# Half-wide moving operands in the levels of a triangular inverse (chunked delta rule, one core)

## The reference

```python
L = jnp.where(strict, jnp.einsum('bhnid,bhnjd->bhnij', k_beta, kc) * decay, 0.0)
T = lax.linalg.triangular_solve(eye + L, jnp.broadcast_to(eye, L.shape),
                                left_side=True, lower=True, unit_diagonal=True)
v_corr = jnp.einsum('bhnij,bhnjd->bhnid', T, v_beta)
k_cumdecay = jnp.einsum('bhnij,bhnjd->bhnid', T, k_beta * jnp.exp(gc)[..., None])
```

## Time and profile before

| | us |
|---|---|
| median of 3 runs | 3319.24 |
| lowest, highest | 3318.76, 3329.38 |
| profiled execution, time | 3317.98 |
| profiled execution, span | 3315.7 |
| PE busy | 3227.7 (97%) |
| PE weight loads busy | 2680.6 (81%) |
| DVE busy | 2195.3 (66%) |
| ACT busy | 773.8 (23%) |

### The profile page before, as it was taken

How to read it: one execution, slowest core, us unless ns; L and a number is a source line. 1 busy time by engine, 2 the same in 40 slices (tenths; PEclk the granted TensorE clock), 3 DMA queues, 4 the chain that set the end, 5 groups by cost and what they waited for, 6 DMA issues and landing times.

```text
span 3315.7 us, 40252 instructions
## 1 busy us (share of the span) xinstructions
PE 3227.7 (97%) x15737; PEld 2680.6 (81%) x15737; DVE 2195.3 (66%) x3316; ACT 773.8 (23%) x1248; POOL 1834.9 (55%) x994
## 2 busy tenths in 40 slices
PE   6999999999999999999999999999999999999999
PEld 5787778887877887888888888888878887888887
DVE  6975389963336257564755888788854337888884
ACT  2152322211224122333121111255531011111110
POOL 4547367766541653012666666633356666777775
PEclk9999999999999999999999999999999999999999
DMA  3223122322320221000333444455553336556662
GB/s 132 84 64 102 53 92 97 96 96 89 111 73 26 94 78 58 14 20 31 119 106 117 140 140 138 134 200 207 204 185 105 123 121 208 186 190 200 199 194 99
DMA packets 164525, 391.67 MB, mean 118 GB/s; under 512 B 10865, under 2 KB 69489, under 8 KB 162289
## 3 DMA queue, kind: packets, MB, share of 16 engines
q1 hardware_dynamic: 73408, 262.70, 24.0%
q10 hardware_dynamic: 90928, 126.39, 11.3%
HBM read 326.14 MB, written 62.91 MB: 117 GB/s over the span
## 4 chain that ended last, share of the span: by engine, by line
PE 84%; DVE 11%; issue 2%; ACT 1%; DMA 1%; POOL 0%; DVEq 0%; ACTq 0%; POOLq 0%
PE banks L1519 22%; PE banks L1521 22%; PE banks L1520 22%; PE banks L909 3%; DVE sb_sq L2226 3%; PE banks L802 1%; PE banks L794 1%; PE banks L378 1%; DVE sb_tmp L2236 1%; DVE sb_sq L2224 1%; PE banks L1581 1%; PE banks L1555 1%; PE banks L1557 1%; PE banks L1556 1%; DVE sb_zL L546 1%
## 5 line engine op out<-in xcount | busy, mean ns | idle before, releaser
L1507 POOL TENSOR_TENSOR sb_wL<-sb_raw,sb_wH 128x1024 fp32r<-128x1024 f32 x495 | 1207.5, 2439 | 1454.1 <-PE banks L1521 1401.8
L1519 PE MATMUL banks<-sb_hH,sb_wH 128*128 128x512 f32 x2040 | 820.0, 402 | 12.9 <-ACT sb_sq L1124 3.1
L1520 PE MATMUL banks<-sb_hL,sb_wH 128*128 128x512 f32 x2040 | 796.7, 391 | 0.0
L1521 PE MATMUL banks<-sb_hH,sb_wL 128*128 128x512 f32 x2040 | 796.6, 390 | 0.0
L1502 POOL TENSOR_SCALAR sb_wH<-sb_raw 128x1024 fp32r<-128x1024 f32 x495 | 643.0, 1299 | 14.9 <-DMA sb_raw<-in_weights 14.9
L1519 PEld LDWEIGHTS banks<-sb_hH,sb_wH 128*128 128x128 f32 x2040 | 384.9, 189 | 97.6 <-issue 12.6
L1521 PEld LDWEIGHTS banks<-sb_hH,sb_wL 128*128 128x128 f32 x2040 | 383.8, 188 | 81.3
L1520 PEld LDWEIGHTS banks<-sb_hL,sb_wH 128*128 128x128 f32 x2040 | 385.0, 189 | 73.2 <-issue 1.7
L1519 PE MATMUL banks<-sb_pzH,sb_wH 128*128 128x512 f32 x1024 | 399.8, 390 | 5.9 <-DVE sb_xT L1471 3.8
L1521 PE MATMUL banks<-sb_pzH,sb_wL 128*128 128x512 f32 x1024 | 398.9, 390 | 0.0
L1520 PE MATMUL banks<-sb_pzL,sb_wH 128*128 128x512 f32 x1024 | 398.9, 390 | 0.0
(11 more groups left out here) (432 smaller groups left out, 4623.6 us busy)
## 6 DMA issues: line engine op xcount, KB each, us to landing
sb_raw<-in_weights SPq DMA_DIRECT2D x495, 512.0 KB, 3.7
gates<-sb_stage ACTq DMA_DIRECT2D x16, 2048.0 KB, 7.8
acts<-sb_sq ACTq DMA_DIRECT2D x96, 256.0 KB, 2.0
sb_Gt<-gates ACTq DMA_DIRECT2D x24, 1024.0 KB, 7.5
sb_Ga<-acts ACTq DMA_DIRECT2D x24, 1024.0 KB, 11.1
sb_Gt<-gates ACTq DMA_DIRECT2D x4, 2048.0 KB, 9.8
sb_xT<-in_xT SPq DMA_DIRECT2D x4, 512.0 KB, 9.9
acts<-sb_xT ACTq DMA_DIRECT2D x1, 2048.0 KB, 7.8
```

The source lines that it names most:

```text
L1507: nc.gpsimd.tensor_tensor(wL[:, t % LOS, :], raw[:, t % RAWS, :], wH[:, t % HIS, :].bitcast(F32), ALU.subtract).then_inc(sems("weights_lo" ...
L1519: pe.matmul(out, hi, H, start=start, stop=False)
L1520: pe.matmul(out, hi, L, start=False, stop=False)
L1521: return pe.matmul(out, lo, H, start=False, stop=stop)
```

## The change

Only half of the columns are now moved through the array in each level. `off_blocks` multiplies only the left columns of each pair of `T` (64 of 128 per head), `updates` only the right columns of `R`, and both write 64 columns a head compactly into one bank (columns 0 to 255 and 256 to 511). ACT copies 256 columns in place of 512, of `X` and of `T`. Since `X` is now only partly written, DVE clears the columns that the next level must find at zero: 128 columns a group in each of levels 1 to 5 ahead of the subtraction, and 256 columns a group in the preparation. In level 1 PE's order is `off_blocks` 0, `updates` 0, `off_blocks` 1, `updates` 1. Weight operands (`N`, `X`) stay 128 x 128.

```diff
+        def of_one(ap, lv, right):
+            return ap.rearrange("p (n h r) -> p n h r", h=2, r=1 << lv)[:, :, right, :]
+        def of_four(ap, lv, right):
+            return ap.rearrange("p x (n h r) -> p (x n) h r", h=2, r=1 << lv)[:, :, right, :]
+        def halves(m, lv, updates, x=None):
+            a, n = (256 * updates, 256) if x is None else (256 * updates + 64 * x, 64)
+            return ps[m][:, a:a + n].rearrange("p (n r) -> p n r", r=1 << lv)
...
-                        out = ps[X_BANK[c]][:, col(x)]
-                        mm = pe.matmul(out, g["N"][:, x], g["T"][:, x], start=True, stop=True) if lv else turn(out, g["N"][:, x])
+                        if lv:
+                            mm = pe.matmul(halves(X_BANK[c], lv, 0, x), g["N"][:, x], of_one(g["T"][:, x], lv, 0), start=True, stop=True)
+                        else:
+                            mm = turn(ps[X_BANK[c]][:, col(x)], g["N"][:, x])
...
-                        mm = pe.matmul(ps[X_BANK[c]][:, col(x)], g["X"][:, x], g["R"][:, x], start=True, stop=True)
+                        mm = pe.matmul(halves(X_BANK[c], lv, 1, x), g["X"][:, x], of_one(g["R"][:, x], lv, 1), start=True, stop=True)
...
                     for c in range(2):
                         off_blocks(lv, c)
-                    for c in range(2):
+                        if lv == 1:
+                            updates(1, c)
+                    for c in range(2 if lv > 1 else 0):
                         updates(lv, c)
...
-                        act.activation(G[c]["X"], bank4(X_BANK[c]), ACT.Copy).then_inc(sems("gd_Xc"), 1)
+                        act.activation(of_four(G[c]["X"], lv, 0), halves(X_BANK[c], lv, 0), ACT.Copy).then_inc(sems("gd_Xc"), 1)
...
-                        act.activation(G[c]["T"], bank4(Y_BANK[c]), ACT.Copy).then_inc(sems("gd_T"), 1)
+                        act.activation(of_four(G[c]["T"], lv, 0), of_four(bank4(Y_BANK[c]), lv, 0), ACT.Copy).then_inc(sems("gd_T"), 1)
...
                     chain(v.tensor_tensor(g["aT"], bank4(3), g["X"], ALU.mult))
+                    v.memset(of_four(g["X"], 1, 1), 0.0)
...
-                        right = lambda ap: ap.rearrange("p x (n h r) -> p (x n) h r", h=2, r=1 << lv)[:, :, 1, :]
+                        R = of_four(G[c]["R"], lv, 1)
                         E.wait("gd_YT")
-                        v.tensor_tensor(right(G[c]["R"]), right(G[c]["R"]), right(bank4(X_BANK[c])), ALU.subtract).then_inc(sems("gd_R"), 1)
+                        if lv < LEVELS - 1:
+                            pairs = G[c]["X"].rearrange("p x (n g h r) -> p (x n) g h r", g=2, h=2, r=1 << lv)
+                            v.memset(pairs[:, :, 1, 0, :], 0.0)
+                        v.tensor_tensor(R, R, halves(X_BANK[c], lv, 1), ALU.subtract).then_inc(sems("gd_R"), 1)
```

## The result

| | before | after |
|---|---|---|
| median of 20 runs, us | 3320.05 | 3334.7 |
| lowest, highest | 3316.68, 3329.75 | 3324.28, 3341.75 |
| profiled execution: time, span | 3317.98, 3315.7 | 3325.69, 3323.4 |
| its granted clock, mean | 0.995 | 0.992 |

The ratio is 1.0038, 95% interval 1.0028 to 1.0048: slower by 0.4%, 14.6 us, where 80 were forecast. The profiled execution lies at the low end of the changed kernel's runs, 7.7 us of span above that of before. The changed kernel's runs spread with their clock: those with a mean clock of 0.992 took 3324.28 to 3325.69 us, those with 0.986 took 3340.83 to 3341.75.

The account below looks back on a forecast made before the run. PE was taken to bound a level: 36 weight-load slots, one product's latency, one ACT copy. At low clock +19.6 us a block, +78.4 for four, plus 1.9 for preparation memsets, gave 3399 us; range 3311 to 3410.

Parts of the forecast that it names:

- the case on which it stood: Levels 1 to 6 of all four blocks: clock stays at 1.2 GHz until the dense products behind; 3399 us, chance 0.50.
- levels 2 to 5: The four steady levels of each block, at low clock: 8.65 us each against 5.03, +14.5 us a block.
- level 6: Last level of each block, at low clock: 32 slots take 6.82 us against 3.7, +3.1 a block.
- returns in mid-block: Rival: clock low in some blocks only, or back in mid-block; 3317 plus 20 for each block, 3337 to 3377, chance 0.10.
- The parts of the cold level: Steady level at low clock: 32 slots 6.82 us, then result, memset, subtraction and `turn_back` 1, ending at 8.65.
- the tail: Low-clock level behind its 32 slots: result 0.35 us, memset 0.165, subtraction 0.42, 0.05 to PE, `turn_back` 1 0.85.
- The slot: PE's time per weight load and product in the levels: still 0.111 us with 64 columns, bounds 0.056 to 0.115.
- The fast rival: Rival: 64-column slots take 0.056 us in the levels, a level about 3.9; 3293 us; both faster ways together 0.05.
- The steady level: Levels 2 to 5 at full clock, in the rival of full-clock terms alone (3317 us, chance 0.35): 4.87 us against 5.03.
- The preparation: DVE's memsets of 256 columns ahead of the levels: 0.27 us each, seven on the path, +1.9 us; 0 if covered.
- Level 1: First level of each block, from `off_blocks` 1 on, at low clock: 6.0 us, -0.2 a block, from -1.0 to +0.5.
- a rival of small chance: Rival: `updates` 0 fills PE's wait in level 1, the clock never falls; 3309 us; both faster ways together 0.05.

Follow-up runs that it names:

- order_only: The kernel before with only level 1's new order (`updates` 0 ahead of `off_blocks` 1), products 128 columns wide; 3315.06 us, ratio 0.9989 to before.
- full_columns: The changed kernel with its copies, memsets and order, but 128 columns in each product of `off_blocks` and `updates`; 3320.53 us, ratio 0.9994 to before.
- before_filled: The kernel before plus three unused products of 512 columns behind `off_blocks` 0 of level 1; 3314.75 us, ratio 0.9982 to before.
- wide_half_copies: The changed kernel with 128-column products, level 1's `X` copied in full and no memset in the preparation; 3318.11 us, ratio 0.9982 to before.

## Why the prediction was wrong

The direction (slower, 0.60) and the range hold; the size does not, and the case on which it stood did not happen. That the direction came out was luck in good part: some 7.5 of the 14.6 us come from a collision that the prediction did not have.

- **The step that failed** is "I take as likeliest that the clock, once at 1.2 GHz in level 1, stays there until the dense 128-column products behind level 6". In the levels it stays low for longer, 6.8 to 13.7 us in the changed kernel's profile and up to 17.1 in its variants', where 128 columns have 3.4 to 6.8, but it returns in level 2 or 3. In the place of 16 cold levels stood one in the profile, and four cold in part. Of the terms, levels 2 to 5 (+14.5 a block) measured +2.80, -0.28, -0.97 and -0.41, and level 6 (+3.1) measured -0.05. The rival "returns in mid-block" at a chance of 0.10, was the right mechanism; at 20 us a block it was priced too high as well.
- **The parts of the cold level were right**: 8.43 against 8.65. Of the 0.22 too much, 0.15 are the slots: 32 took 6.67 us (1318.86 - 1312.19), 0.208 each and not 0.213. The other 0.07 are the tail, 1.76 against 1.83: I put group 1's subtraction on the path, and `turn_back` 0 covers it, as the eight loads of `turn_back` run without a gap in 1.72.
- **The slot** was right: 0.112 with 64 columns. The fast rival at 0.056 is out. It rested on a reading of the Trainium skill (TensorE: Matmul & The Clock Gate, "Back-to-back issue gap") that the section does not bear: it gives its about 60 cycles for products of up to 64 columns as the gap of isolated products, says that this leaves out the load, and that in a stream of loads and products both set the spacing. The trace agrees with the latter: for these float32 products, each with its own weight load, the slot is 0.112 us.
- **The steady level** at full clock was 4.77 against 4.87: memset and subtraction overlap, and the subtraction is shorter out of the compact bank.
- **The preparation** was the other term that was mis-sized: +1.9 in the prediction, +10.0 measured, or 7.5 with the 2.5 that the wait ahead of `off_blocks` 1 gave back. "They are on the path" was right and the durations were right (0.27). What was missed is who is met 0.1 us later: the row of POOL's split, 0.10 us behind `N`, stood in the trace of before.
- **Level 1** (-0.2 a block, within -1.0 to +0.5) measured -0.43, -1.14, +0.30, -0.10, one of them just outside, from `off_blocks` 1 to level 2. The forecast kept PE's wait as a cold one in every case but a rival of small chance; order_only shows that the order alone keeps the clock up with 128 columns, in three of four blocks. Why it does not with 64 in the changed kernel is shown only as far as full_columns goes: by the narrow products.

What stays open is what decides, from one execution to the next, whether the clock returns after 6.8 or 17.1 us; the medians carry it, and one profile of each kernel does not show it.

## What to carry to other kernels

Narrower moving operands gained next to nothing here, 0.3 us in a block of 60, where each product loads its own 128 x 128 float32 weights, and they cost clock where PE came out of a wait; look at the granted clock of the stretch first, and fill such a wait, with useful products or with unused ones. Before an instruction is put into a gapless run of DVE, list what POOL starts within some tenths of a microsecond of each later DVE instruction with two SBUF inputs: a start of 0.1 us behind instead of ahead cost 2.1 us here. Where a kernel's runs spread by 17 us, one profile explains its own run, and a term must be tested by medians of variants.

## What was not expected of the hardware

- A DVE step of 0.69 us takes 2.81 if POOL's 128 x 1024 step with two SBUF inputs started 0.10 us earlier, and 0.69 if it starts 0.10 us later; POOL then takes 2.81 in place of 2.36.
- Unused products are worth their place: 3 of 512 columns a block, 2.74 us of PE's time in a wait, made the kernel before 0.2% faster.
- After a wait of PE, in the profiled levels, the clock came back out of 64-column products in 6.8 to 17.1 us and out of 128-column ones in 3.4 to 6.8. Elsewhere it stayed low for 17.1 and 20.5 us in gapless work that mixed 512-column with one-column products (before_filled, full_columns and wide_half_copies).
